# A transformer step on one core: more jobs in flight in attention, another SiLU, fillers and small vector work moved, three expert loads together

## The chip, the cores and the metric

The kernel runs on one core of one Trainium2 chip. The core has TensorE (PE), VectorE (DVE), ScalarE (ACT), GpSimd (POOL) and SyncE (SP, which issues most DMAs), sixteen DMA engines, an on-chip memory with 128 partitions, and eight accumulator banks that TensorE writes. The metric is the device time of one launch in microseconds (us).

## What is computed

One layer of a hybrid decoder in float32, for a prompt of 512 tokens and 8 sequences of 4 new tokens (32 "sample" tokens; 544 in all), model width 1024. The parts that the change touches:

```python
mod = (c @ w_ada + b_ada)[:, None, :]
sh1, sc1, gt1, sh2, sc2, gt2 = jnp.split(mod, 6, axis=-1)
h = x * (1.0 + sc1) + sh1
(qkv_a, z_a, b_a, a_a, q_b, k_b, v_b, f_b, g_a, g_b) = _split_cols(h @ w_in, IN_SIZES)
out = xp[:, 0:n] * w[0]                      # _causal_conv, 4 taps, 1536 channels
for i in range(1, CONV_WIDTH):
    out = out + xp[:, i:i + n] * w[i]
return jax.nn.silu(out), xp[:, n:]
...
q_a = _l2norm(q_a.reshape(hs)) * GDN_HEAD_DIM ** -0.5
k_a = _l2norm(k_a.reshape(hs))
o_a, ssm_new = _gdn_chunked(q_a, k_a, v_a, beta, g, ssm0.astype(f32), chunk)
o_a = _rmsnorm(o_a, norm_g.astype(f32)) * jax.nn.silu(z_a.astype(f32).reshape(hs))
o_b = _fox_prompt(q_b, k_b, v_b, logf)       # softmax(q.k/sqrt(d) + F_t - F_s), causal, 8 heads
merged = jax.nn.sigmoid(g_a) * (o_a @ w_ba) + jax.nn.sigmoid(g_b) * (o_b @ w_bb)
x = _layernorm(DEEPNORM_ALPHA * x + gt1 * (merged @ w_out), ln1_g, ln1_b)
h2 = x * (1.0 + sc2) + sh2
ffn = _moe(h2, ...)                          # 64 experts, top 8 by groups, and a shared one
x = _layernorm(DEEPNORM_ALPHA * x + gt2 * ffn, ln2_g, ln2_b)
```

## The kernel before

The program is a sequence of stages (blocks); in each, every engine has a list of work of its own, and counters (semaphores) join them. An engine runs its list in order, so what stands first in a list holds what stands behind it.

- **FoX prompt (163.5 to 340 us).** 32 jobs (`JOBS`), one per query block t and head h. `scores(j)` writes a bank (two score banks, 0 and 1), VectorE adds the mask and takes the row maximum (L789, L790), ScalarE does the exponential (L812), TensorE transposes the result (L727), ScalarE copies that back, and TensorE multiplies by v. Scores run two jobs ahead (`scores(j + 2)`). Between them TensorE makes the projection for the convolution's channel blocks (`projection`, L615), one of 128 channels every four jobs. For block m, ScalarE copies the input halves (`conv_in`, L659 to L661), VectorE runs the taps in four parts during the next four jobs (`conv_part`, L680 to L686), ScalarE applies SiLU in the last of these (`conv_silu`, L663 to L667), TensorE transposes the rows at job 4m + 1 of two blocks later (`conv_rows`), and VectorE takes them (`take_rows`). These products go through three banks in turn (5, 6, 7). In iteration j, VectorE's list is: maximum of j, then a convolution part.
- **FoX sample (340 to 487.5).** Attention of the sample tokens over cached pages.
- **Norms (487.5 to 511.8).** VectorE squares and sums q and k of the convolution, ScalarE takes a root, VectorE scales; TensorE has a few small products and the transposes of the convolution's state.
- **GDN (511.8 to 868).** Four blocks t of 128 tokens. Each: four transposed operands (L1251, copied by L1421), decay rows, an inverse in six levels l (`NL`), and the state update. TensorE's waits are filled with 80 "later pieces" (`later_pieces`): halves over k of the products for the branch gates ga and gb (L1196, eight matmuls each), and rows for the second modulation. Each place in the list takes a fixed count of them: two before the state, one after the transposes, one per level and two at l = 4, and so on, 20 per block. Their weights come in twelve loads of 2 MB ("slabs", `load_later` and `send_later`) into two slots; ScalarE copies each result (`later_out`) and stores the gates in DRAM. GpSimd and VectorE also run the sample tokens' recurrence here, until about 700.
- **Gated norm (868 to 887.5).** VectorE normalises and gates, TensorE transposes (L1561). The weights of both branches, x and half of the out-projection weights are asked for at its start (L1575 to L1579).
- **Branches (887.5 to 958).** For 8 blocks m of 128 channels, TensorE makes branch product a and b (16 matmuls each, L429) into four pairs of banks, ScalarE applies the sigmoid to gates read back from DRAM (L1695; two buffers), VectorE multiplies (L1722 to L1724). Ahead of m = 2 stands `later_modulation` (L1705 to L1709 for prompt and sample, ten operations) and three small ones.
- **Out-projection, layernorm, routing, shared expert (958 to 1134).** VectorE adds biases to two pairs of gate rows (L2337) ahead of its first layernorm, whose first reading of the out-projection is L2341.
- **Experts (to 1720).** 64 experts by rank of load in groups ("units"), weights of 3 MB each in four slots (`load_by_rank`), gathered rows, `gate_up` (L1846) and `down_half` (L1854). SyncE asks for rank 0, waits for the lists and the first gather, and asks for ranks 1 and 2.

## Time and profile before

| | us |
|---|---|
| median of 3 runs | 1792.89 (1791.1 to 1795.9) |
| the profiled execution | 1793.59 |
| its span, first to last instruction | 1791.8 |
| TensorE busy | 1585.4 (88%) |
| VectorE busy | 655.8 (37%) |
| ScalarE busy | 331.0 (18%) |
| GpSimd busy | 311.4 (17%) |
| mean granted TensorE clock, share of 2.4 GHz | 0.937 |

The profile is one execution; its times are us from the first instruction. The table of stretches gives busy times, the clock and the DMA share per stage; the list of waits and a line's own rows say for what an engine stood idle; the timeline joins equal instructions in a row into one line with their count. The idle time before an instruction and what ended it stand in brackets. The granted clock has two levels here, 1.00 (2.4 GHz) and 0.50 (1.2 GHz); a number between is a mean.

### The profile page before, as it was taken

Reading aid. Unit: us, or ns where it says so; the run is one execution under the profiler, and the core shown is the slowest. Engines: PE = TensorE matmul, PEld = TensorE weight load, DVE = VectorE, ACT = ScalarE, POOL = GpSimd, SP = SyncE. Lnnn points to the kernel's source line nnn. Section 1 sums busy time; section 2 is a strip of 40 time slices with the busy share of each in tenths; the row PEclk is TensorE's granted clock in tenths of the full one; section 3 lists DMA queues with packets and bytes.
Section 4 is the critical chain, followed back from the end, with each engine's and each line's share of the span. In section 5 each row is a group of like instructions: output and inputs, shape, how many; then the busy total and the mean of one; then the engine's idle time right before and its main releaser. Section 6 shows DMA issues by size and latency. Waiting matters only on the chain. (4 is left out here: it accounts for less than half of the span.)

```text
span 1791.8 us, 20650 instructions
## 1 busy us (share of the span) xinstructions
PE 1585.4 (88%) x7886; PEld 908.6 (51%) x7886; DVE 655.8 (37%) x1245; ACT 331.0 (18%) x662; POOL 311.4 (17%) x328
## 2 busy tenths in 40 slices
PE   5998888999957989999687998889989999998966
PEld 2856665664446767778474543333433434343322
DVE  2001333343278393533453884341111111111128
ACT  1001233433222121212110130011111111111120
POOL 5000000000029992000000052111111111111000
PEclk8997899999978999999798998999999999999988
DMA  9213110112141223321654002999999999999856
GB/s 340 91 47 101 26 48 1 48 48 79 70 108 38 81 87 105 113 86 44 228 195 159 35 16 75 368 422 405 419 414 419 381 404 422 397 418 420 346 206 261
DMA packets 111678, 357.13 MB, mean 199 GB/s; under 512 B 36011, under 2 KB 36139, under 8 KB 85459
## 3 DMA queue, kind: packets, MB, share of 16 engines
q1 hardware_dynamic: 88582, 304.08, 44.1%
q0 software_dynamic: 14384, 35.89, 5.1%
q10 hardware_dynamic: 8614, 15.84, 2.5%
q8 instruction: 64, 1.05, 0.3%
q14 instruction: 34, 0.28, 0.0%
HBM read 330.70 MB, written 37.64 MB: 206 GB/s over the span
## 5 line engine op out<-in xcount | busy, mean ns | idle before, releaser
L1846 PE MATMUL bank<-arena 128*32 128x512 f32 (+2 forms) x1536 | 336.2, 616 | 27.9 <-DMA arena<-in_w_up 27.7
L1846 PEld LDWEIGHTS bank<-arena 128*32 128x32 f32 (+2 forms) x1536 | 121.2, 138 | 210.4 <-issue 210.4
L1854 PE MATMUL bank<-arena 128*32 128x512 f32 (+2 forms) x768 | 168.7, 598 | 0.7 <-DVE arena L2540 0.7
L1196 PE MATMUL bank<-arena 128*128 128x272 f32 x512 | 129.4, 403 | 20.2 <-PEq L1058 19.2
L2534 DVE TENSOR_TENSOR arena<-arena,bank 128x256 f32<-128x256 f32 x46 | 19.4, 421 | 331.2 <-ACT arena L2212 331.2
L437 PE MATMUL bank<-arena 128*128 128x512 f32 (+4 forms) x384 | 126.8, 490 | 9.8 <-DVE arena L2341 7.5
L429 PE MATMUL bank<-arena 128*128 128x272 f32 x512 | 124.1, 407 | 11.3 <-DVE arena L1723 5.4
L1833 POOL DMA_INDIRECT expert_rows<-arena x46 | 46.4, 1008 | 482.0 <-PE bank L1839 427.0
L429 PEld LDWEIGHTS bank<-arena 128*128 128x128 f32 x512 | 101.0, 198 | 33.7 <-issue 6.1
L1196 PEld LDWEIGHTS bank<-arena 128*128 128x128 f32 x512 | 95.4, 193 | 44.5 <-issue 21.8
L1854 PEld LDWEIGHTS bank<-arena 128*32 128x32 f32 (+2 forms) x768 | 54.9, 134 | 110.7 <-issue 109.8
L615 PE MATMUL bank<-arena 128*128 128x272 f32 x384 | 108.1, 430 | 0.0
L437 PEld LDWEIGHTS bank<-arena 128*128 128x128 f32 (+1 forms) x384 | 60.7, 192 | 74.0 <-issue 65.3
L615 PEld LDWEIGHTS bank<-arena 128*128 128x128 f32 x384 | 76.4, 209 | 18.5 <-issue 3.6
L2212 ACT ACTIVATE arena<-bank 128x256 f32<-128x256 f32 x46 | 17.7, 384 | 353.6 <-PE bank L1846 353.6
L1356 DVE TENSOR_TENSOR arena<-arena 128x512 f32<-128x512 f32 x48 | 78.2, 1630 | 1.6
L2546 DVE COPY arena<-bank 128x512 f32<-128x512 f32 x46 | 31.8, 691 | 128.0 <-PE bank L1854 128.0
L1490 POOL TENSOR_TENSOR arena<-arena 128x512 f32<-128x512 f32 x5 | 6.8, 1354 | 344.3 <-POOLq L1058 344.0
L2270 POOL DMA_INDIRECT expert_lists<-arena x34 | 35.5, 1045 | 159.2 <-DVE arena L2394 149.8
L1280 PE MATMUL bank<-arena 128*128 128x128 f32 x320 | 47.4, 308 | 11.9 <-DVE arena L1391 7.9
L1829 POOL DMA_INDIRECT arena<-h_rows,arena x46 | 46.5, 1012 | 55.7 <-PE bank L1970 30.3
L2218 ACT COPY arena<-bank 128x512 f32<-128x512 f32 x46 | 27.0, 587 | 148.9 <-PE bank L1854 148.9
(427 smaller groups left out, 2084.3 us busy)
## 6 DMA issues: line engine op xcount, KB each, us to landing
arena<-in_w_gate SPq DMA_DIRECT2D x64, 1024.0 KB, 13.4
arena<-in_w_up SPq DMA_DIRECT2D x64, 1024.0 KB, 17.7
arena<-in_w_down SPq DMA_DIRECT2D x64, 1024.0 KB, 15.4
arena<-in_w_ada SPq DMA_DIRECT2D x12, 2048.0 KB, 9.3
arena<-in_w_in SPq DMA_DIRECT2D x11, 2048.0 KB, 9.1
arena<-expert_rows SPq DMA_DIRECT2D x8, 2048.0 KB, 25.8
gate_logits<-arena ACTq DMA_DIRECT2D x16, 272.0 KB, 3.3
arena<-gate_logits SPq DMA_DIRECT2D x8, 544.0 KB, 5.7
```

Of the source, the lines that this page charges most:

```text
L429: mm = nc.tensor.matmul(pair[i][:, 0:HALF], w[:, k, m * P:(m + 1) * P], rhs[:, k, i * HALF:(i + 1) * HALF], start=k == 0, stop=k == kt - 1)
L437: mm = nc.tensor.matmul(out, lhs[:, k, t * P:t * P + n], w[:, k, cols], start=k == 0, stop=k == kt - 1)
L615: mm = nc.tensor.matmul(out[:, 0:HALF], w[:, k, (m % 4) * P:(m % 4 + 1) * P], hT[:, k, half * HALF:(half + 1) * HALF], start=k == 0, stop= ...
L1196: mm = nc.tensor.matmul(out[:, 0:HALF], w[:, k, m * P:(m + 1) * P], hT[:, k, half * HALF:(half + 1) * HALF], start=k == 0, stop=k == KD - 1)
L1280: mm = nc.tensor.matmul(bank[hb][:, col(h)], Lm[:, h, :], Tm[:, h, :], start=True, stop=True)
L1356: done(lm_done, nc.vector.tensor_tensor(Lm_of[l % 2][:, hs, :], LT[:, hs, :], lvl[:, l, :].unsqueeze(1).to_broadcast([P, 4, P]), ALU.mult))
L1829: return nc.gpsimd.indirect_dma_start(out=into, out_offset=None, in_=h2_d, in_offset=bass.IndirectOffsetOnAxis(ap=rows, axis=0), bounds_ch ...
L1833: return nc.gpsimd.indirect_dma_start(out=y_d, out_offset=bass.IndirectOffsetOnAxis(ap=rows, axis=0), in_=of, in_offset=None, bounds_check ...
L1846: mm = nc.tensor.matmul(out[rows].rearrange("p (a n) -> p a n", a=2), x[:, k, rows], gate_up_slot(n)[:, :, k, :], start=k == 0, stop=k == ...
L1854: mm = nc.tensor.matmul(out[rows, :], h[:, k, rows], down_slot(n)[:, k, 512 * half:512 * half + 512], start=k == 0, stop=k == 1)
L2270: scat.inc(nc.gpsimd.indirect_dma_start(out=list_rows, out_offset=bass.IndirectOffsetOnAxis(ap=adi[:, t, k:k + 1], axis=0), in_=tokval[:, ...
L2546: nc.vector.tensor_copy(Yb[u % RY][:, 512:D], bank[6][:, :]).then_inc(y_v.sem, 1)
```

## The change

1. FoX prompt: three score banks (0, 1, 7), scores three jobs ahead; the other products go through two banks. The SiLU of blocks 0 to 5 is made as (tanh(y) + 1) · y with y half the convolution: ScalarE halves the taps of these blocks once and runs a tanh, VectorE multiplies. Block 6 keeps SiLU, at the stage's end. `conv_rows` moves one job on.
2. Norms: this block now holds 12 of the 80 pieces, and SyncE sends slab 2 from there, behind a wait for slab 1's last piece. The GDN blocks lose three pieces each.
3. Branch b's weights are loaded during GDN, and its products m = 0 and 1 are made in the gated-norm stage.
4. `later_modulation` is split into six portions, one behind each of m = 1 to 6.
5. The second pair of gate biases is added behind the second layernorm.
6. The loads of ranks 1 and 2 follow rank 0's at once.

```diff
+    conv_e, conv_th = at(T2 + 6096, TOK), Tick(nc, "conv_tanh")
+    HALVED = len(JOBS) // 4 - 2
+    def conv_tanh(act, m):
+        act.wait_ge(conv_sum.sem, m + 1)
+        if m:
+            act.wait_ge(conv_act.sem, m)
+        ach.inc(nc.scalar.activation(conv_e[:, 0:SEQ], post[m % 2], ACT.Tanh))
+        conv_th.inc(nc.scalar.activation(conv_e[:, SEQ:TOK], post_s[:, m, :], ACT.Tanh))
+    def conv_gate(dve, m):
+        step = chained(dve, vch)
+        dve.wait_ge(conv_th.sem, m + 1)
+        step(nc.vector.scalar_tensor_tensor(post[m % 2], conv_e[:, 0:SEQ], 1.0, post[m % 2], ALU.add, ALU.mult))
+        done(conv_act, nc.vector.scalar_tensor_tensor(post_s[:, m, :], conv_e[:, SEQ:TOK], 1.0, post_s[:, m, :], ALU.add, ALU.mult))
...
-    RING = (5, 6, 7)
+    RING, SB = (5, 6), (bank[0], bank[1], bank[7])
...
             for j, (t, h) in enumerate(JOBS):
-                if j + 2 < len(JOBS):
-                    scores(j + 2)
+                if j + len(SB) < len(JOBS):
+                    scores(j + len(SB))
...
-                if j % 4 == 1 and m >= 2:
+                if j % 4 == 2 and m >= 2:
                     conv_rows(pe, m - 2, RING)
...
                 if m >= 1:
                     conv_part(dve, m - 1, j % 4)
+                if m >= 2 and j % 4 == 1:
+                    conv_gate(dve, m - 2)
                 if m >= 2 and j % 4 == 3:
                     take_rows(dve, m - 2)
...
+            taps = histT[:, 0:HALVED, NH:NH + CONV]
+            hist_half.inc(nc.scalar.mul(taps, taps, 0.5))
...
-                if j % 4 == 3 and m >= 1:
-                    conv_silu(act, m - 1)
+                if j % 4 == 0 and m >= 2:
+                    conv_tanh(act, m - 2)
                 if t and h == 4:
                     take_oT(t - 1)
             take_oT(PT - 1)
+            conv_silu(act, HALVED)
...
             cn_mm.inc(mm)
+            later_pieces(pe, "squares", 6)
+            later_pieces(pe, "norms", 6)
...
+            later_out(act, "squares")
             act.wait_ge(g_sb.sem, 1)
...
             sq_root.inc(nc.scalar.activation(ss, ss, ACT.Sqrt))
+            later_out(act, "norms")
...
             load_later(sp, 1)
+            sp.wait_ge(fill_mm.sem, slab_end[1])
+            load_later(sp, 2)
             sp.wait_ge(ab_done.sem, 1)
...
-                later_pieces(pe, (t, "state before"), 2)
+                later_pieces(pe, (t, "state before"), 1)
...
                 tr_mm.inc(mm)
-                later_pieces(pe, (t, "transposes"), 1)
                 pe.wait_ge(tr_sb.sem, t + 1)
...
-                    later_pieces(pe, (t, l), 2 if l == NL - 2 else 1)
+                    later_pieces(pe, (t, l), 1)
...
+            sp.wait_ge(stored.sem, stored.n)
+            branch_in[1].inc(sp.dma_start(wbb, A["w_branch_b"][0].rearrange("(k p) n -> p k n", p=P)), 16)
             for j in range(8, len(LATER)):
                 send_later(j)
...
                 n = TOKS[t]
+                if t == 0:
+                    pe.wait_ge(branch_in[1].sem, 16)
+                    yb_mm.inc(feature_major(wbb, 0, oTb, bank[4:6], CW))
+                    yb_mm.inc(feature_major(wbb, 1, oTb, bank[6:8], CW))
                 pe.wait_ge(on_done.sem, t + 1)
...
-            pe.wait_ge(branch_in.sem, 32)
+            pe.wait_ge(branch_in[0].sem, 16)
             for m in range(KD):
                 for w, tick, free, rhs, b0 in ((wba, ya_mm, ta_done, oTa, 0), (wbb, yb_mm, tb_done, oTb, 4)):
+                    if w is wbb and m < 2:
+                        continue
...
             for m in range(KD):
-                if m == 2:
-                    later_modulation()
...
                 step(nc.vector.tensor_tensor(mT[:, m, :], ta, tb, ALU.add))
+                if 1 <= m <= 6:
+                    later_modulation(m - 1)
+            sample_token_values()
...
             load_by_rank(sp, 0)
-            sp.wait_ge(lists_in.sem, 16)
-            sp.wait_ge(g_ld[0].sem, 16)
             load_by_rank(sp, 1)
             load_by_rank(sp, 2)
...
-                    for load, gate, bias in ((gtb_load, gtb, b_gt), (gt2_load, gt2b, b_gt2)):
-                        dve.wait_ge(load.sem, 48)
-                        for i, m in enumerate((P, NS_TOK)):
-                            done(gt_ready, TT(gate[0:m, i], gate[0:m, i], bias[0:m], ALU.add))
+                    add_gate_bias(gtb_load, gtb, b_gt)
...
             layernorm(1)
+            add_gate_bias(gt2_load, gt2b, b_gt2)
             choose(0)
```

A portion of `later_modulation` is two, two and one operations, first for the prompt rows and then for the sample rows.

## Rows read from the trace of the kernel before

**Rows 1.** Stages: length, busy time (instructions) of each engine, granted clock, DMA share, GB/s.
```profile
163.50:340.00 176.50, 156.32 (x676) 110.15 (x676) 59.39 (x148) 63.43 (x161) 3.79 (x12) 0.90 0.12 35
...
511.80:614.00 102.20, 87.97 (x584) 70.30 (x585) 69.62 (x57) 20.68 (x37) 84.94 (x51) 0.92 0.28 78
...
707.00:787.00 80.00, 77.58 (x577) 62.10 (x576) 33.83 (x56) 19.19 (x36) 0.00 (x0) 1.00 0.39 114
...
887.50:958.00 70.50, 63.02 (x256) 51.00 (x256) 32.66 (x53) 10.18 (x9) 2.76 (x16) 0.93 0.50 177
...
1134.00:1720.00 586.00, 553.32 (x2756) 228.49 (x2756) 114.65 (x287) 71.07 (x137) 89.47 (x89) 0.98 0.97 394
```

**Rows 2.** Page, section 5: line, operation, count, busy, mean ns, idle before.
```profile
L1846 PE MATMUL bank<-arena 128*32 128x512 f32 (+2 forms) x1536 | 336.2, 616 | 27.9 <-DMA arena<-in_w_up 27.7
```

**Rows 3.** Waits of TensorE from 163.5 to 340: total us, times, longest.
```profile
PE bank L727 <- ACT arena L812: 17.7, 7, 3.4
```

**Rows 4.** Timeline, FoX prompt stage: start us, us, engine, line, operation [idle before, releaser].
```profile
201.25 0.36 ACT L659 COPY arena<-bank 128x240 f32<-128x240 f32 x1 [4.13 <-PE bank L615]
...
203.81 0.42 DVE L790 TENSOR_REDUCE arena<-bank 128x1 f32<-128x256 f32 x1
...
204.16 1.28 ACT L812 ACT_TABLE_LOAD   x1
...
205.45 0.47 ACT L812 ACTIVATE arena<-bank,arena 128x256 f32<-128x256 f32 x1
...
206.07 0.69 PE L727 MATMUL bank<-arena 128*128 128x128 f32 x2 [3.44 <-ACT arena L812]
...
320.28 0.69 DVE L790 TENSOR_REDUCE arena<-bank 128x1 f32<-128x512 f32 x1
...
322.00 0.69 ACT L812 ACTIVATE arena<-bank,arena 128x512 f32<-128x512 f32 x1
```

**Rows 5.** Table by stretch again, behind the gap that ends at 206.07.
```profile
204.90:211.70 6.80, 5.63 (x16) 4.40 (x16) 1.89 (x5) 2.21 (x7) 0.00 (x0) 0.50 0.03 2
```

**Rows 6.** Timeline, end of the norms stage and start of the GDN stage.
```profile
504.91 6.26 DVE L1094 TENSOR_TENSOR arena<-arena 128x1024 f32<-128x1024 f32 x5
...
511.70 5.79 PE L1196 MATMUL bank<-arena 128*128 128x272 f32 x16 [19.22 <-PEq L1058]
```

**Rows 7.** Timeline, GDN: a later piece in block three, transposes of four.
```profile
755.79 3.83 PE L1196 MATMUL bank<-arena 128*128 128x272 f32 x16
...
792.73 2.05 PE L1256 MATMUL bank<-arena 8*128 8x128 f32 x16 [0.69 <-ACT arena L1421]
...
794.71 3.14 PE L1259 MATMUL bank<-arena 64*128 64x256 f32 x16
```

**Rows 8.** Timeline, branch stage (887.5 to 958).
```profile
887.47 0.88 SPq L1676 DMA_DIRECT2D arena<-gate_logits  x2
...
901.75 1.11 ACT L1695 ACTIVATE arena<-arena 128x1088 f32<-128x1088 f32 x1 [7.59 <-DMA arena<-gate_logits]
...
910.07 1.22 DVE L1705 TENSOR_TENSOR arena<-arena 128x1024 f32<-128x1024 f32 x1
...
924.16 31.74 PE L429 MATMUL bank<-arena 128*128 128x272 f32 x128 [5.36 <-DVE arena L1723]
```

**Rows 9.** Timeline, start of the out-projection stage.
```profile
970.53 2.47 DVE L2337 TENSOR_TENSOR arena<-arena 128x1024 f32<-128x1024 f32 x2 [12.84 <-DMA arena<-in_b_ada]
...
978.12 2.47 DVE L2337 TENSOR_TENSOR arena<-arena 128x1024 f32<-128x1024 f32 x2 [5.12 <-DMA arena<-in_b_ada]
...
981.37 16.56 PE L437 MATMUL bank<-arena 128*128 128x512 f32 x32 [7.50 <-DVE arena L2341]
...
998.04 0.69 DVE L2341 TENSOR_TENSOR arena<-bank,arena 128x512 f32<-128x512 f32 x1 [4.30 <-PE bank L437]
```

**Rows 10.** Before the experts: one stretch of the table, one row of SyncE's timeline.
```profile
1100.00:1120.00 20.00, 19.17 (x44) 6.87 (x42) 4.70 (x13) 1.31 (x4) 0.00 (x0) 0.93 0.00 1
...
1152.73 0.34 SPq L1762 DMA_DIRECT2D arena<-in_w_gate  x1
```

218 lines of the change are left out of this document (115 added, 103 removed).

## The prediction

> **What bounds the kernel now.** I read the table of stages first. In the FoX prompt stage (163.5 to 340) TensorE works 156.3 of 176.5 us at a mean clock of 0.90 [rows 1]: it sets the pace, so every gap in it is time, and so is its lower clock level. In the first GDN block (511.8 to 614) it works 88.0 of 102.2 us beside 69.6 us of VectorE and 84.9 us of GpSimd; in the third (707 to 787) it works 77.6 of 80.0 [rows 1]. So the first two blocks are set by chains between engines, and the last two by TensorE's own amount of work. The branch stage has 63.0 us of TensorE in 70.5 us. The experts stage moves data at a DMA share of 0.97, and TensorE waits there 27.7 us for weights [rows 1, 2]: transfers set it. Then I read the waits of TensorE, and a timeline around each.
>
> **FoX prompt stage.** TensorE waits seven times, 17.7 us, for an exponential [rows 3]. The timeline shows one. ScalarE copies the convolution's second input half at 201.25, VectorE starts that block's convolution from it (four operations) and only then takes the row maxima, whose end is 204.23. The exponential starts at 205.45, because the SiLU and two table loads stand before it; TensorE resumes at 206.07 after a gap of 3.44 us [rows 4]. The change takes the tables away: 205.45 − 204.23 less 0.04 of issue, 1.18 us here; in the last one 322.00 − 320.97 less 0.04, 0.99 [rows 4]. Over the six such places I get 5.85 us (0.47 to 1.26 each). The rest stays. Scores three jobs ahead do not shorten it, since the maxima still stand behind the convolution's first part in VectorE's own order, and this waits for ScalarE's copy. So gaps of 0.7 to 2.3 us remain.
>
> The gaps also cost clock. In 204.9 to 211.7, behind this one, the granted clock was 0.50, the 1.2 GHz level [rows 5]; six such stretches (3.4 us each but this) add to about 24 us, 12 us lost. The last gap of this kind, the shortest, was followed by none. I expect three of the six to remain, a gain of 6 to 8: 7 us. Against it: a row copy of 0.69 us and its wait now share an interval with a softmax maximum, 1 us; and the seventh block's SiLU stands alone at the end, 1.28 + 0.63 + 0.21, 2.1 us. The new VectorE work (0.74 + 0.25 per block) lies in intervals of some 5 us in which VectorE was a third busy [rows 1]. Halving the taps is one small ScalarE operation before any use. Sum: 5.9 + 7 − 1 − 2.1 = 10 us gain. Bounds: 4, if all clock stretches remain, and 14, if none does.
> The Trainium skill, "ScalarE: Activation LUTs", What ACT_TABLE_LOAD costs, puts each switch at 1283 ns plus a drain, together about 2.66 us; by it six places would give up to 8 us more, and the stage 18. The trace does not agree: the load of 204.16 takes 1.28 us and the exponential starts 0.01 us behind it [rows 4].
>
> **Norms and GDN.** TensorE stood idle for 19.22 us until 511.70, while VectorE went through the norms until 511.17, and the first two pieces then took 5.79 us at the low level, where 16 of them take 3.83 warm [rows 6, 7]. Twelve pieces now go in front: ten gate halves of eight matmuls at 1.83 (the 3.83 for 16, less the last one's drain), and a modulation product of eight with its single-matmul row piece, taken as 2.8 together; 21.1 us, plus 1.7 for a cold start, from 492.5. That ends at 515.3, 3.6 us after 511.7. ScalarE's root is 1 us later behind piece copies, so VectorE ends at 512.2, still first. The slab asked for at 487.5 lands after 11.6 us, in time for the fifth piece. SyncE now waits there for a slab's end before it sends its small stores; they land under these same pieces.
> What comes out of the GDN blocks is worth less than its length. The piece behind the transposes was wholly hidden: TensorE ended it and still waited 0.69 us for ScalarE's four copies [rows 7]. A piece alone lasts 2.0 with its drain, so without it the wait is 2.7 us, four times, at no time of its own. The second piece at the fifth level gives 1.83 in the last two blocks (TensorE-bound), nothing in the first two. One "state before" piece gives 1.0 in each of the last two, 2.3 in the first (5.79 becomes about 2.9 and the scaled rows are ready at 3.3), 0 in the second: 8.0 us. Idle of 2.7 us can drop the clock: for two or three of the four stretches, 1.7 us each, as in the last block, where L1259 took 3.14 us for 16 matmuls behind even the 0.69 us gap [rows 7], 4.1 in all. Net 3.9, so both stages together 3.9 − 3.6, about 0. Bounds −5 (clock drops at every shorter filler) and +5 (none).
> In SyncE's queue the branch-b weights (2 MB, landing in 9 us like the slabs there) now stand before slab 8. That slab then lands about 8 us before its first piece needs it: 0.
>
> **Gated norm.** TensorE has 14 us of idle there, up to 879.1. Two branch-b products take 2 × 16 × 0.23 = 7.4 us, up to 10.7 cold, from 868: they end beside the first transpose. I take 0.3 lost, bounds 0 and 1.
>
> **Branch stage.** Eight products run from the stage's start at 887.5, then TensorE waits 5.36 us until 924.16 for VectorE, which went through ten modulation operations of 1.2 us from 910.07; the other eight take 31.74 us, 1.7 of it for a cold start, so a product warm is 3.7 [rows 8]. The cause ahead of that is a DMA backlog: the first gates, asked for at 887.47, let ScalarE go on at 901.75 [rows 8], 14.3 us later, behind four loads of 2 MB. Now: two branch-a products, 7.4 us; 2 MB less are queued, 5 us, so the gates land 9 us into the stage; sigmoid and two products 2.0, so TensorE resumes at 11.1. Then twelve products of 3.7, 44.4; clock 1.7; end 2.1: 59.3 instead of 70.5, 11 us gained. Modulation portions (two operations, 2.5 us) beside a 2.6 us turn of VectorE fit into 7.4 us per channel group. If their inputs land late (VectorE would wait for them in its second turn), there are some 8 us before TensorE notices. Bounds: 9 (gates at their old delay of 14) and 15.5 (gates at once, warm).
>
> **Out-projection.** VectorE had the first gate bias pair done at 973.0, waited 5.12 us for the second load until 978.12 and added it until 980.6; only then it read the out-projection's banks, and TensorE resumed after a gap of 7.50 us, with 32 matmuls in 16.56 us, cold, where 13.7 is the warm time (32 at some 0.43). VectorE waited for them at 998.04 [rows 9]. With the second pair moved behind, the layernorm starts 7.6 us earlier, TensorE goes on without a gap and warm, and the bank that VectorE read at 998.04 is ready by 987.5: 10.2 us earlier. The pair itself costs 2.47 later, in a chain of VectorE that has no gaps from there: 7.7 us gained. Bounds 5 and 9.
>
> **Experts.** DMA rests from 1100 to 1120 [rows 10], when two experts more could be loading. But expert 4's load waits for a free slot until 1152.73 [rows 10], and the transfers in flight then had only 4.6 us to go. Anything earlier than that makes the DMA idle before 1152.7 instead: 4 us gained, bounds 2 and 5. The loads might delay small gathers of the routing; at 15 us of transfer in a 20 us hole they end first.
>
> **Sum.** 10 + 0 − 0.3 + 11 + 7.7 + 4 = 32.4 us. The profiled execution has a span of 1791.8 and took 1793.59; the median of the runs is 1792.9, 0.7 lower. 1793.6 − 32.4 = 1761.2.
>
> **Rivals.**
> (a) The moved pieces were the cover in GDN: TensorE gains nothing in the last two blocks and each of the four transposes and several levels drop the clock, and the FoX stage keeps all its stretches: 5 + 6 less, 1772. For it: 16.56 against 13.7 [rows 9] shows how dear a cold start is. Chance 0.13.
> (b) The pieces count fully: all twelve, 21 us out and 3.6 in, 17 gained: 1744. Against it: the 0.69 us of waiting behind the hidden piece. Chance 0.10.
> (c) The third score bank removes the whole wait in the FoX stage: 17.7 of gaps and 12 of clock, less 3: 27, 17 more than forecast, 1744. Against it: VectorE's order. Chance 0.08.
> (d) Tanh needs a table of its own, so that the loads stay: the stage loses 3 instead of gaining 10: 1774. No row shows a tanh. Chance 0.03. The Trainium skill, same page, Table sets, lists tanh in the exponential's set; no trace so far shows it.
> (e) Slower: with fillers gone from GDN, TensorE falls to the low level behind the transposes and does not come up again between the many short waits of the levels. At that level work takes twice as long (3.4 us of one stretch lose 1.7), so the sum is eaten up from 65 us spent there more than before; with a third of the four blocks (119 us) it costs 59: 1821. For it: the clock of the first block is already 0.92 [rows 1]. Against it: the third block ran at 1.00 with only one piece per level. Chance 0.04. The Trainium skill, "TensorE: Matmul & The Clock Gate", What's actually happening, says that the low level is the default and activity releases it, which speaks for such a fall; rows 5 agree, in 3 to 7 us pieces.
> (f) The gates or the modulation inputs come late, branch stage gains only 5: 1767. Chance 0.05.
>
> **How the numbers follow.** The forecast has the rest, 0.57, and its own range from the bounds is 1751 to 1772. With (a), (d), (f) above and (b), (c) below, 8 in 10 lie in 1743 to 1775. A measurement of this kernel tells from no change what is beyond 0.3%, 5.4 us. Faster by more: 0.95, within: 0.02, slower: 0.03.
>
> **What would show it.** FoX stage: no table loads but at its end, waits of TensorE for exponentials near 12 us in all, clock near 0.94. Norms stage some 27.9 us long. In GDN, waits of 2.7 us behind the transposes, and the first block no shorter than 98. Branch stage 57 to 60, one wait of TensorE near its start. Out-projection stage shorter by 7 to 8, no cold run of 32 matmuls. Load 4 issued with the DMA nearly idle. The prediction is wrong if GDN falls in clock, if VectorE's order does not hold the maxima, or if the gates land as late as before.

## The result and the profile after

The changed kernel takes 1784.95 us (1780.21 to 1785.43), the kernel before 1794.3 in the same set: a ratio of 0.9939, 95% interval 0.9922 to 0.9956. In two later sets with the same pair it was 0.9918 (0.9889 to 0.9947) and 0.9919 (0.9892 to 0.9945). So the change gains 0.6 to 0.8%, 9 to 13 us by the medians. I had forecast 1761.2, in a range of 1743 to 1775: the sign holds, the size is 0.3 to 0.4 of the 32.4 us forecast, and the time lies outside the range.

The profiled execution of the changed kernel (span 1783.4, 8.4 less than before) by stages. Columns as in rows 1; the stages are in order FoX prompt, FoX sample, norms, GDN, gated norm, branches, out-projection and routing, experts, end:

```profile
162.85:342.69 179.84, 162.96 (x676) 114.47 (x677) 64.72 (x160) 48.16 (x150) 3.78 (x12) 0.86 0.13 41
342.69:489.99 147.30, 146.32 (x652) 75.99 (x652) 46.65 (x123) 44.91 (x80) 0.00 (x0) 0.98 0.16 54
489.99:517.26 27.27, 26.43 (x130) 18.93 (x130) 20.67 (x22) 8.26 (x17) 0.00 (x1) 0.94 0.54 184
517.26:875.64 358.38, 312.19 (x2190) 249.17 (x2190) 186.44 (x217) 75.58 (x138) 150.72 (x89) 0.92 0.25 80
875.64:893.93 18.29, 13.19 (x52) 9.76 (x52) 14.45 (x22) 4.13 (x7) 0.00 (x1) 0.78 0.97 346
893.93:954.16 60.23, 55.15 (x225) 44.38 (x225) 32.67 (x53) 10.18 (x9) 2.76 (x16) 0.95 0.52 176
954.16:1125.23 171.07, 153.29 (x508) 70.53 (x509) 110.20 (x273) 26.48 (x44) 38.09 (x39) 0.94 0.33 121
1125.23:1707.51 582.28, 553.30 (x2750) 227.41 (x2748) 112.43 (x283) 69.83 (x136) 88.26 (x88) 0.98 0.95 389
1707.51:1783.40 75.89, 47.60 (x105) 19.40 (x104) 46.57 (x59) 12.54 (x39) 0.97 (x1) 0.83 0.67 270
```

Here and in the table below a stage runs from its first computing instruction to that of the next. In the same measure the kernel before has 177.2, 146.8, 24.2, 357.6, 18.1, 70.7, 178.0, 581.7 and 73.9. The differences are +2.6, +0.5, +3.0, +0.8, +0.2, −10.5, −6.9, +0.6 and +2.0; with 0.7 ahead of the first stage they make the 8.4. Two stages, branches and out-projection, gave nearly what was forecast (−11 and −7.7). The FoX prompt stage was to give 10 and cost 2.6; norms and GDN cost 3.8 where 0.3 was to be gained; the experts were to give 4 and gave nothing. These are differences of two profiles; the table of all runs below shows how far a stage moves with its code unchanged.

### The profile page after: what moved, and what is told of

It reads as the page before. It is cut to its first block and busy times, and to the rows that moved or that the text cites. A ratio compares the mean times of both kernels' runs of the same rounds, so it can differ in the third digit from the quotient of the medians.

```text
span 1783.4 us, 20662 instructions
## 1 busy us (share of the span) xinstructions
PE 1604.6 (90%) x7886; PEld 922.7 (52%) x7886; DVE 656.0 (37%) x1257; ACT 315.6 (18%) x651; POOL 310.3 (17%) x328
## 5 line engine op out<-in xcount | busy, mean ns | idle before, releaser
L429 PE MATMUL bank<-arena 128*128 128x272 f32 x512 | 125.5, 409 | 12.8 <-PEq L1272 4.3
L1130 PE MATMUL bank<-arena 128*128 128x272 f32 x512 | 128.5, 400 | 0.6 <-ACT arena L1166 0.6
L618 PE MATMUL bank<-arena 128*128 128x272 f32 x384 | 111.4, 440 | 0.0
L1390 DVE TENSOR_TENSOR arena<-arena 128x512 f32<-128x512 f32 x48 | 69.1, 1439 | 1.6
L1314 PE MATMUL bank<-arena 128*128 128x128 f32 x320 | 44.6, 295 | 10.6 <-DVE arena L1425 6.6
## 6 DMA issues: line engine op xcount, KB each, us to landing
arena<-in_w_up SPq DMA_DIRECT2D x64, 1024.0 KB, 17.7
```

What stands on the lines that cost most here:

```text
L429: mm = nc.tensor.matmul(pair[i][:, 0:HALF], w[:, k, m * P:(m + 1) * P], rhs[:, k, i * HALF:(i + 1) * HALF], start=k == 0, stop=k == kt - 1)
L618: mm = nc.tensor.matmul(out[:, 0:HALF], w[:, k, (m % 4) * P:(m % 4 + 1) * P], hT[:, k, half * HALF:(half + 1) * HALF], start=k == 0, stop= ...
L1130: mm = nc.tensor.matmul(out[:, 0:HALF], w[:, k, m * P:(m + 1) * P], hT[:, k, half * HALF:(half + 1) * HALF], start=k == 0, stop=k == KD - 1)
L1314: mm = nc.tensor.matmul(bank[hb][:, col(h)], Lm[:, h, :], Tm[:, h, :], start=True, stop=True)
L1390: done(lm_done, nc.vector.tensor_tensor(Lm_of[l % 2][:, hs, :], LT[:, hs, :], lvl[:, l, :].unsqueeze(1).to_broadcast([P, 4, P]), ALU.mult))
```

## Where the FoX prompt stage's gain went

The list of TensorE's waits in that stage of the changed kernel has, as the answer to rows 3:

```profile
PE bank L746 <- ACT arena L833: 11.6, 11, 2.3
...
PE bank L738 <- ACT arena L664: 1.2, 3, 0.6
```

17.7 us have become 12.8: at the six places 7.6 us of waiting went away, and seven new waits of 0.2 to 0.6 us brought 2.7 back. The 5.9 us forecast for the tables came in as 4.9. The timeline at the place of rows 4 shows how:

```profile
203.53 0.43 DVE L809 TENSOR_REDUCE arena<-bank 128x1 f32<-128x256 f32 x1
...
203.99 0.47 ACT L833 ACTIVATE arena<-bank,arena 128x256 f32<-128x256 f32 x1 [2.19 <-DVE arena L809]
...
204.61 0.69 PE L746 MATMUL bank<-arena 128*128 128x128 f32 x2 [2.25 <-ACT arena L833]
...
204.71 0.64 ACT L677 ACTIVATE arena<-arena 128x512 f32<-128x512 f32 x1
205.09 3.83 PE L618 MATMUL bank<-arena 128*128 128x272 f32 x8
```

The exponential now starts 0.03 us behind the maximum (203.96) and ScalarE is idle before it; the gap is 2.25 instead of 3.44, to 0.01 the 2.26 worked out. Between this exponential and the tanh at 204.71 there is no table load. The Trainium skill, "ScalarE: Activation LUTs", Table sets, has the exponential and tanh in one set; the trace agrees, with no load in the 0.72 us between the two starts.

But the projection's eight matmuls at 205.09 still take 3.83 us. The table of stretches for the granted clock:

```profile
203.80:217.50 13.70, 12.89 (x34) 9.38 (x34) 5.22 (x13) 3.41 (x12) 0.00 (x0) 0.50 0.03 2
...
289.10:292.60 3.50, 3.50 (x11) 2.55 (x9) 0.00 (x0) 0.00 (x0) 0.00 (x0) 0.51 0.00 0
296.00:302.80 6.80, 5.54 (x18) 4.61 (x18) 5.46 (x12) 3.15 (x8) 0.00 (x0) 0.50 0.01 2
```

The stretch at 1.2 GHz behind the gap at 206 was 6.8 us long before [rows 5]; behind the shorter gap it is 13.7 us in this profile. That length isn't a property of the change: the same code has it in two profiles (changed and yg_undo, described below), and in the five others the stretch is 3.5 us or less, as in control2, the changed kernel unedited in another set:

```profile
206.50:210.00 3.50, 3.12 (x8) 2.51 (x9) 2.69 (x7) 1.65 (x7) 0.00 (x0) 0.51 0.04 2
```

What six of the seven share is elsewhere. The low stretches near 250 and 300 last some 7 us where before they lasted 3 to 3.5, and three stand where before had none: near 290, near 323, and some 2 us at the stage's end. Of the six that I wanted to get rid of, one, near 273, is gone. At 289.1 the level fell while TensorE was busy: its last wait had ended 16 us earlier. The stage's mean clock is 0.86 against 0.90 [rows 1]. For the same 676 matmuls TensorE is busy for 163.0 us against 156.3 (160.1 to 162.8 in the six other profiles), and it stands idle for 16.9 us against 20.9. So the idle time shrank by 4.0 us, and the busy time grew by 4 to 7.

## The experiments

Each kernel is the changed kernel with one edit, unless it says otherwise. Stage lengths are of its profile, in us; "low" is 2 × (1 − mean clock) × length of the FoX prompt stage, the time at 1.2 GHz that its mean clock stands for (this counts also the stage's start, low for its first 10 to 11 us, in control and best2 for 17). Each stage length is of one profile: a difference of 3 us in the FoX prompt stage is within what the same code shows.

| kernel | FoX prompt (low) | norms + GDN | branches | out-proj., routing | experts | ratio to before (95%) |
|---|---|---|---|---|---|---|
| before | 177.2 (35) | 381.8 | 70.7 | 178.0 | 581.7 | 1 |
| changed | 179.8 (50) | 385.6 | 60.2 | 171.1 | 582.3 | 0.9939 (0.9922, 0.9956) |
| control | 179.7 (50) | 385.6 | 59.8 | 177.8* | 582.0 | 0.9918 (0.9889, 0.9947) |
| control2 | 177.3 (43) | 385.7 | 59.4 | 171.1 | 582.1 | 0.9919 (0.9892, 0.9945) |
| silu3 | 187.2 (56) | 383.1 | 59.8 | 179.8* | 586.1 | 0.9911 (0.9883, 0.9940) |
| tanh2 | 179.8 (47) | 383.8 | 59.9 | 179.5* | 585.3 | 0.9919 (0.9891, 0.9946) |
| a_undo | 186.0 (52) | 382.8 | 59.6 | 179.7* | 582.7 | 0.9949 (0.9929, 0.9969) |
| a_undo2 | 176.9 (35) | 384.0 | 59.3 | 170.3 | 585.1 | 0.9904 (0.9874, 0.9934) |
| silu3_rb | 178.2 (43) | 383.1 | 59.5 | 170.0 | 585.1 | 0.9895 (0.9852, 0.9939) |
| d_undo | 176.9 (42) | 379.2 | 59.9 | 180.4* | 582.3 | 0.9882 (0.9852, 0.9911) |
| d_keep | 177.0 (42) | 379.0 | 60.2 | 180.4* | 582.0 | 0.9892 (0.9866, 0.9917) |
| hf_undo | 177.2 (43) | 385.6 | 69.2 | 178.1* | 582.4 | 0.9943 (0.9922, 0.9964) |
| yg_undo | 178.3 (43) | 382.7 | 64.0 | 176.3 | 585.0 | 0.9996 (0.9980, 1.0012) |
| projfirst | 162.0 (19) | 384.2 | 59.5 | 180.0* | 583.3 | 0.9867 (0.9824, 0.9909) |
| before_pf | 157.8 (19) | 378.9 | 71.8 | 178.4 | 582.1 | 0.9878 (0.9841, 0.9914) |
| best | 161.7 (19) | 363.9 | 59.7 | 170.5 | 582.5 | 0.9755 (0.9723, 0.9786) |
| best2 | 167.4 (30) | 365.1 | 60.0 | 170.1 | 582.0 | 0.9760 (0.9727, 0.9793) |
| pf_silu | 161.6 (26) | 376.5 | 62.1 | 170.3 | 583.3 | 0.9762 (0.9735, 0.9789) |

The star marks profiles with a stall of 6.3 us of TensorE at one place of the routing, told of at the end. The runs were made in five sets, each with the kernel before in it, the last four on four different chips. The stall came in all eight kernels of the second and third set and in none of the other profiles, and the kernel before took 1805.1 and 1803.9 us there, 1794.3 to 1796.4 in the other sets. So kernels are compared by total only within a set or by their ratio, and by this stage only with or without the stall.

**control.** The changed kernel, unedited.

> The changed kernel once more, unedited, on the chip of the three that follow, to know which of its stages hold still. The first profile had 179.8 us in the FoX prompt stage and 171.1 in the out-projection and routing stage; four edited kernels whose edits lie elsewhere had 177.0 to 187.2 and 179.5 to 180.4 there. Theory A (these stages differ by where thin stretches and instruction supply fall, not by the edits): one of the two moves here by 3 us or more. Theory B (the edits moved them): both repeat within 1 us.

FoX prompt repeated (179.7), the routing stage was 6.7 us longer, by the stall. So theory A, for one of the two stages. That FoX prompt came out equal is luck: here the start was low for 17 us instead of 10, and the stretch behind the gap at 206 lasted 3.5 instead of 13.7.

**control2.** The same in the last set.

> The changed kernel once more beside these: FoX prompt stage 177.0-179.8, out-projection and routing 171 or 178, ratio to before 0.989-0.996.

All three expectations held. FoX prompt 177.3: the same code of this stage has 176.9 to 179.8 in seven profiles (changed, the two controls, d_undo, d_keep, hf_undo, yg_undo).

**silu3** and **tanh2**, the two sides of the stage's change:

```diff
-                if m >= 2 and j % 4 == 1:
-                    conv_gate(dve, m - 2)
...
-                if j % 4 == 0 and m >= 2:
-                    conv_tanh(act, m - 2)
+                if j % 4 == 3 and m >= 1:
+                    conv_silu(act, m - 1)
```
```diff
-    RING, SB = (5, 6), (bank[0], bank[1], bank[7])
+    RING, SB = (5, 6, 7), (bank[0], bank[1])
```

> The changed kernel with the SiLU of the kernel before (on ScalarE, with its two table loads per block) and whole taps, but three score banks and scores three jobs ahead. The FoX prompt stage took 177.2 us before and 179.8 in the changed kernel, although TensorE waited 5.3 us less. Theory A (the tanh shortens the waits, something else costs clock): waits of TensorE for exponentials go back from 11.6 to 16-18 us, and the low clock (24 us before, 40 in the changed kernel) stays near 40 if the third score bank and the pair of banks for the rest cause it: stage 183-187. Theory B (the tanh with VectorE's extra work is what costs clock): low clock back to some 24 us, stage 176-178.

> The changed kernel with two score banks, scores two jobs ahead, and three banks in turn for the rest, as before; the tanh stays. Theory A (third score bank costs the clock): waits for exponentials near 12 us, low clock at or under 24 us, stage 168-173 us. Theory B (the tanh costs it): low clock near 40 us, stage 178-181. Theory C (the clock falls by where a thin stretch of TensorE's work happens to lie, no part of the change owns it): somewhere between, 172-178, and silu3 between as well.

With SiLU the stage is 187.2, low 56, and the waits for exponentials are 17.5 us: theory A's numbers, so the tanh isn't what costs clock. (This profile is the longest of silu3's four executions, 1799.5 us, where the others took 1785.3 to 1791.1; so 187.2 may be high.) Yet without the third bank (tanh2) it is 179.8 with 47: not its theory A, 168 to 173, but theory B's number, 178 to 181, by which the tanh costs the clock. The two answers contradict each other as long as tanh and bank are the only suspects. What the two kernels have in common is `conv_rows` one job later.

**a_undo** undoes both at once but leaves `conv_rows` in its new place; **a_undo2** moves this back as well; **silu3_rb** moves it back with three score banks:

```diff
-                if j % 4 == 2 and m >= 2:
+                if j % 4 == 1 and m >= 2:
                     conv_rows(pe, m - 2, RING)
```

> The changed kernel with the FoX prompt stage of before: two score banks, three banks in turn, SiLU; all else changed. Theory A (the stage's changes gave nothing, the clock took it back): stage 176-178, total within 3 us of the control. Theory B (the stage as changed is worth 3-7 us and the first profile was unlucky): total 3-7 us above the control. The banks for scores, changed alone with SiLU, gave 187.2; with both undone the stage must be back at some 177.

> The changed kernel with the FoX prompt stage wholly as before: SiLU, two score banks and also conv_rows one job earlier, which the run a_undo had left in its new place. That one took 186.0 us, with 52 us of low clock, where before has 177.2 with 35, with the same seven waits. Theory A (the place of the row transposes decides how much low clock this stage has with SiLU): 177 us and 35 again. Theory B (the clock falls by the stage's start in time, whatever the order): 182 or more, or a number between.

> The changed kernel with SiLU and conv_rows in its old place, but with three score banks and two banks in turn for the rest. With SiLU and two score banks the stage has 176.9 us (35 us of low clock) with conv_rows in its old place and 186.0 (52) with it one job later; with three score banks and conv_rows later 187.2 (56). Theory A (the place of the row transposes costs it, the third bank nothing): 176-179 us, low 33-40. Theory B (two banks in turn instead of three also cost): 182-188.

a_undo missed its text: the stage should have been back at 177 and took 186.0. By the total it is theory B, 5.1 us above the control. a_undo2 is theory A, 176.9 and 35. silu3_rb is theory A by its length, 178.2, with 43 of low clock, above the 33 to 40 expected. The two FoX prompt stages, first a_undo, then a_undo2 (the stretches), then the waits for exponentials of both:

```profile
162.80:348.80 186.00, 163.57 (x676) 115.21 (x677) 59.40 (x148) 63.80 (x161) 3.78 (x12) 0.86 0.12 35
```
```profile
162.79:339.64 176.85, 155.63 (x676) 109.79 (x677) 59.39 (x148) 63.81 (x161) 3.79 (x12) 0.90 0.12 37
```
```profile
PE bank L745 <- ACT arena L830: 19.2, 11, 3.4
```
```profile
PE bank L745 <- ACT arena L830: 17.7, 7, 3.4
```

One line moved costs 9.1 us: 7.9 are TensorE's busy time at the lower clock, 1.5 are four new waits of 0.2 to 0.6 us. The seven waits that both have agree to 0.01 us, and both stages start at 162.8 (theory B, the stage's start in time, is out). silu3 against silu3_rb is the same edit with three score banks, and shows 9.0. The totals say so less sharply: 0.9949 against 0.9904 for the first pair, 0.9911 against 0.9895, within their intervals, for the second.

Where the clock goes can be seen in a_undo:

```profile
299.20:316.40 17.20, 17.20 (x55) 11.55 (x55) 2.80 (x6) 2.79 (x7) 0.00 (x0) 0.70 0.00 1
```

TensorE is busy all of this time, and yet the level is low in three parts of it, until 302.8, from 306.3 to 309.5 and from 312.9 to 316.3. In a_undo2 the same work, with four transposes of `conv_rows` in it, runs at the full clock from 299.3 on.

So in the order in which it can be built the stage's change splits into the third bank, +1.3 (not told from noise), the row transposes later, +9.0, and the tanh, −7.3 to −10.2 (silu3 to the changed kernel's 179.8 to 176.9; −6.2 from a_undo to tanh2). The tanh needs the later place, because its rows are finished one job later, on VectorE. So the price of the place is measured with SiLU; that it is the same with the tanh isn't shown. Nor is it settled why the level falls again and stays low longer with the row transposes there.

**projfirst.** What the wait needs is other work:

```diff
+                m = j // 4
+                if j % 4 == 0:
+                    projection(pe, m, 0, 0, RING)
                 if j + 1 < len(JOBS):
                     prob_transposes(j + 1)
-                m = j // 4
-                projection(pe, m, j % 4 // 2, j % 2, RING)
+                if j % 4:
+                    projection(pe, m, j % 4 // 2, j % 2, RING)
```

> The changed kernel with one order changed: in every fourth job of the FoX prompt stage TensorE makes the projection's eight matmuls (2 us) ahead of the transposes of the next job, in the place where it waits for the exponential behind VectorE's first convolution part. Theory A (VectorE's order holds the maximum, and the wait only needs other work): the waits of 2.3, 2.3, 2.1 and 1.9 us there vanish, low clock falls from 42-50 us to 15-25, stage 164-170 us. Rival (the low clock comes from thin work such as transposes and 64-column matmuls, not from the waits): the waits vanish and the low clock stays above 35 us, stage 172-175.

162.0 us, low 19: theory A, 2 us below its range. Its timeline at the place shown above, and its waits:

```profile
201.36 2.10 PE L618 MATMUL bank<-arena 128*128 128x272 f32 x8
...
202.61 0.42 DVE L812 TENSOR_REDUCE arena<-bank 128x1 f32<-128x256 f32 x1
...
203.06 0.47 ACT L836 ACTIVATE arena<-bank,arena 128x256 f32<-128x256 f32 x1 [2.19 <-DVE arena L812]
...
203.68 0.44 PE L746 MATMUL bank<-arena 128*128 128x128 f32 x2 [0.22 <-ACT arena L836]
```
```profile
PE bank L746 <- ACT arena L836: 5.3, 10, 1.2
```

The same eight matmuls stand in the gap, at the full clock (2.10 us instead of 3.83), and 0.22 us of it are left. The rival, by which the low clock comes from thin work and not from the waits, wanted 172 to 175 us with more than 35 us low, and is out as the main cause; that the level also falls without a wait is the row of a_undo above.

**before_pf** is the kernel *before* with this edit alone.

> The kernel before with one edit: the projection's eight matmuls ahead of the transposes in every fourth job. Nothing of the change is in it. Theory A (the wait had to be filled, not shortened): FoX prompt stage 161-163 us (177.2 before), other stages as before (GDN 354-360, branches 70-71, out-projection 177-180), ratio to before 0.990-0.993. Rival (part of the 15 us came from tanh or from the third bank): stage 165-170.

```profile
161.26:319.10 157.84, 150.60 (x676) 104.62 (x676) 59.40 (x148) 63.74 (x161) 3.78 (x12) 0.94 0.14 42
```

157.8 us and a ratio of 0.9878, both below theory A's ranges: one reordered call in the kernel before does more than the whole change (0.9919 in the same set; before_pf's four executions took 1771.2 to 1778.2 us, control2's five 1781.3 to 1784.3). With the wait filled, tanh, third bank and the moved rows together are worth nothing: 161.7 and 162.0 with all three (best, projfirst), 157.8 and 161.6 with the stage's code as before (before_pf and, below, pf_silu). Those two have the same code there, so 4 us apart is noise. best2, with the tanh and without the third bank, has 167.4.

**d_undo** and **d_keep**, the later pieces:

```diff
-            later_pieces(pe, "norms", 6)
+            later_pieces(pe, "norms", 2)
...
                 tr_mm.inc(mm)
+                later_pieces(pe, (t, "transposes"), 1)
```

(this is d_keep; ScalarE's `later_out` for the piece comes back with it, and d_undo has all 80 pieces in GDN.)

> The changed kernel with the later pieces as before: none in the norms stage, 20 per GDN block. Norms 27.3 now, GDN 358.4 now; before 24.2 and 357.6. Theory A (pieces moved out of GDN bought nothing there because the clock fell behind the uncovered transposes): norms 24.2, GDN 356-359, in all 3-5 us less than the changed kernel, and low-clock stretches behind the transposes of blocks 2 and 3 gone (17 us at 617-634 and 7 us at 719-726 now). Rival (the clock moves by chance with the start of each stage): GDN anywhere from 353 to 364, with low stretches of 10 us or more in block 2 or 3 too.

> The changed kernel with 8 instead of 12 pieces in the norms stage, and one piece again behind each of the four transposes of GDN (state-before 1, fifth level 1, as in the changed kernel). Theory A (the cover behind the transposes holds the clock): norms 24-25 us, GDN 349-354, in all 8 us or more less than the changed kernel's 385.7. Rival (pieces count by their length wherever they stand): GDN 365, norms 24-25, in all 4 us more.

Both stages together: 379.2, 379.0, and 385.6 for the change. d_undo is theory A, and better than its ranges (GDN 354.6, 6.4 us less in all): the 17 us stretch in block 2 is 7 us long, and the one in block 3 is gone. Over all runs the two stages with the changed pieces have 382.7 to 385.7 us (eleven profiles), with the pieces as before 378.9 to 381.8 (before, before_pf, d_undo). d_keep's total of 6.6 us less misses the 8 of its theory A; its rival had 4 more. The third block's transposes in the changed kernel, then in d_keep:

```profile
714.48 1.94 PE L1286 MATMUL bank<-arena 128*128 128x128 f32 x16 [0.75 <-DVE arena L1443]
716.45 2.44 ACT L1455 COPY arena<-bank 128x512 f32<-128x512 f32 x4 [2.30 <-PE bank L1286]
718.94 3.55 PE L1290 MATMUL bank<-arena 8*128 8x128 f32 x16 [2.52 <-ACT arena L1455]
722.42 3.77 PE L1293 MATMUL bank<-arena 64*128 64x256 f32 x16
```
```profile
713.25 2.00 PE L1130 MATMUL bank<-arena 128*128 128x272 f32 x8
713.45 2.44 ACT L1456 COPY arena<-bank 128x512 f32<-128x512 f32 x4 [2.24 <-PE bank L1286]
715.94 2.05 PE L1291 MATMUL bank<-arena 8*128 8x128 f32 x16 [0.69 <-ACT arena L1456]
717.92 2.00 PE L1294 MATMUL bank<-arena 64*128 64x256 f32 x16
```

The wait of 2.5 us is there as forecast (2.7), and behind it the next 32 matmuls take 7.3 us instead of 4.1: 3.2 for one uncovered place. The third and the fourth block, first of the control, then of d_keep:

```profile
714.00:793.20 79.20, 74.63 (x540) 60.20 (x540) 33.10 (x54) 18.30 (x34) 0.00 (x0) 0.96 0.20 67
793.20:875.20 82.00, 73.73 (x540) 58.28 (x540) 29.63 (x49) 18.40 (x35) 0.00 (x0) 0.92 0.12 43
```
```profile
711.50:787.50 76.00, 73.28 (x548) 59.23 (x548) 33.10 (x54) 18.30 (x34) 0.00 (x0) 1.00 0.32 116
787.50:866.40 78.90, 72.50 (x548) 57.29 (x548) 29.64 (x49) 18.69 (x35) 0.00 (x0) 0.96 0.13 45
```

3.2 and 3.1 us less with eight matmuls *more* in each: theory A for GDN (352.5, within its range). The 5.9 us that GDN gains from changed to d_keep are these two blocks; the first two together have 197.1 in the control and 197.6 in d_keep. The norms stage was off: 26.5, not 24 to 25. VectorE ended at 511.78 there and the next stage began at 513.9, because SyncE waits for the slab's last piece before it sends the small stores for which the stage's end waits. I had named that queue and put it at nothing; with twelve pieces it is covered by their own length. In best, below, the stores go first, and the stage is 25.1.

**hf_undo** puts the ten modulation operations back in one block and the two waits back ahead of expert ranks 1 and 2.

> The changed kernel with two parts undone in stages far apart, each read by its own stage: the ten modulation operations stand again in one block ahead of the third channel group of the branch stage (60.2 us in the changed kernel), and expert ranks 1 and 2 are again asked for only after the lists and the first gather. Branch stage: if VectorE's block was worth what I put it at, 5.4 us or more, it is 65-67; if the earlier gates and weights did the whole, 60-62. Experts (582.3 and 582.0 to 582.3 in kernels on the same chip as it): theory A (expert 4's load, held by its slot, sets the pace, so the early loads bought nothing) within 1 us of the control; theory B (they bought the 4 us forecast) 585-587.

```profile
925.83 24.36 PE L429 MATMUL bank<-arena 128*128 128x272 f32 x92 [8.33 <-DVE arena L1770]
```

The branch stage is 69.2, above both expectations: the block costs 9.4 us against the control, not 5.4. With the gates earlier TensorE runs into it sooner and waits 8.33 instead of 5.36 [rows 8]. Experts: the two kernels have

```profile
1131.09:1713.04 581.95, 553.16 (x2750) 227.62 (x2748) 112.44 (x283) 69.82 (x136) 88.31 (x88) 0.98 0.96 389
```
```profile
1138.86:1721.26 582.40, 551.33 (x2750) 226.91 (x2748) 112.47 (x283) 69.82 (x136) 88.30 (x88) 0.98 0.97 395
```

(control, then hf_undo): 0.4 us apart. Theory A. Over all runs this stage has 581.7 to 582.4 us with the loads as before (before, before_pf, hf_undo) and 582.0 to 586.1 with the early loads (fifteen profiles): never less. The loads were early in the changed kernel, and then the transfers rested:

```profile
1133.00:1143.00 10.00, 9.07 (x45) 3.48 (x43) 1.54 (x3) 0.97 (x2) 0.00 (x0) 1.00 0.32 108
```
```profile
1143.48 0.34 SPq L1808 DMA_DIRECT2D arena<-in_w_gate  x1
```

Expert 4's load is issued 16.5 us after the first expert's matmul in before, control and hf_undo alike, and 18.3 after it in the changed kernel's first profile. In the code this load waits for the unit that last used its slot, however early the data came.

**yg_undo** puts branch b's first two products back into the branch stage and the second gate bias back ahead of the first layernorm.

> The changed kernel with two parts undone, each read by its own stage: branch b's first two products stand again in the branch stage (their weights still come early), and the second pair of gate biases again ahead of the first layernorm. Branch stage 59.8 in the control: the two products cost 7.4 us of TensorE, but this fills the wait for the gates; theory A (the gates hold the start) 59.8 plus 3-5; rival (all of the 7.4 shows) 67. Out-projection and routing stage 171 to 180 in six runs with the change: by its beginning alone (the wait of 7.5 us and the cold 16.6 us) undone it is 7 us longer up to the second layernorm, which is what I read.

```profile
955.02 13.97 PE L437 MATMUL bank<-arena 128*128 128x512 f32 x32 [2.70 <-PEq L1673]
978.19 7.32 PE L437 MATMUL bank<-arena 128*128 128x512 f32 x13 [9.20 <-DVE arena L2382]
```

Branch stage 64.0, 3.8 to 4.6 more than in the three profiles of the changed kernel: theory A. The gap in the out-projection is back, 9.2 us long, and the stage 5.2 to 6.3 us longer than in the seven profiles with the change and without the stall; I had expected 7. By its total (0.9996) nothing is left of the gain: these two parts are worth as much as the whole change.

**best** joins projfirst and d_keep, and sends the small stores ahead of SyncE's wait:

```diff
-            sp.wait_ge(fill_mm.sem, slab_end[1])
-            load_later(sp, 2)
             sp.wait_ge(ab_done.sem, 1)
...
             stored.inc(sp.dma_start(A["conv_sample"][0].rearrange("b i c -> (b i) c"), cnew_rows[n:n + NH, :]), 16)
+            sp.wait_ge(fill_mm.sem, slab_end[1])
+            load_later(sp, 2)
             sp.wait_ge(stored.sem, stored.n)
```

> The changed kernel with three edits together: the projection ahead of the transposes in every fourth job (FoX prompt stage 162.0 us alone, 177 to 180 without), one piece again behind the four transposes of GDN and 8 instead of 12 in the norms stage (379.0 us for both stages, 385.6 without), and SyncE sends the small stores of the norms stage ahead of its wait for the slab (in the run with 8 pieces the next stage began 2 us after VectorE's last operation). Theory A (each holds in its own stage): FoX 162, norms 24.5-25, GDN 352-353, ratio to the kernel before 0.977-0.981. Rival (moving stages against each other moves the clock, so that gains do not add): one of the three is 4 us or more worse than alone.

> The kernel called best with two score banks and three banks in turn for the rest. Theory A (the third score bank is worth nothing): FoX prompt stage 161-163 us and a ratio within 0.5% of best's 0.9755. Rival (it lets the scores pass a wait): stage 165 or more.

> The kernel called best with the whole FoX prompt stage as before the change (SiLU, two score banks, conv_rows one job earlier), but with the projection ahead of the transposes. It prices what tanh and the third bank are worth once the wait has other work in it. By the rows of before the wait was 3.4, 2.8, 2.9, 2.2, 2.4, 1.7 us; 2.0 us of matmuls in front leave 1.4, 0.8, 0.9, 0.2, 0.4, 0. Theory A (tables still cost what is left): stage 165-170. Rival (the tanh and the bank are worth nothing once the wait is filled): 161-164.

best takes 1749.93 us (1745.87 to 1755.24) beside 1795.85 for before: 0.9755 (0.9723 to 0.9786), below the 0.977 to 0.981 of its theory A. It beats both kernels. FoX prompt 161.7 and norms 25.1 are as expected; GDN is 338.9 where 352 to 353 was expected, 13.4 us less than in pf_silu (352.2), which has the same GDN code:

```profile
163.94:325.68 161.74, 151.10 (x676) 105.20 (x676) 64.72 (x160) 48.23 (x150) 3.78 (x12) 0.94 0.14 45
473.76:498.85 25.09, 19.92 (x105) 14.47 (x105) 20.67 (x22) 6.91 (x14) 0.00 (x0) 0.93 0.55 186
498.85:837.70 338.85, 305.02 (x2216) 243.58 (x2216) 182.23 (x217) 76.69 (x141) 148.89 (x89) 0.96 0.28 86
```

The 13 us lie in the first two blocks, where VectorE and GpSimd work at once: they take 185.5 us in best and 198.9 in pf_silu; the last two take 153.3 in both. d_keep, with the same GDN code, is like pf_silu (352.5), best2 like best (340.5). So no edit in GDN made it. The profile of best is its shortest execution and that of pf_silu its longest (1759.8 us, the others 1753.0), and by their medians the two are 3 us apart. best2's FoX prompt stage took 167.4, the number of its rival; some 3 us of its distance to best are a start low for 17 us, which the unedited control has too, and whether the third bank is worth the rest beside the tanh stays open. By its total, 0.9760, best2 isn't told apart from best. pf_silu gave 161.6: the rival's number, tanh and bank together are worth nothing in a filled wait.

## Why the prediction was wrong, point by point

Against the forecast the profile is 24.0 us short (8.4 instead of 32.4). The FoX prompt stage makes 12.6 of it, the experts 4.6, norms and GDN 3.8, the branches and the out-projection 1.3, and the rest, 1.7, lies almost all in stages that were not to change.

- **Tables out of the wait (5.9).** Right in size: 17.7 became 12.8, and the gap at the place shown 2.25, as worked out. That VectorE's order holds the rest was right as well.
- **Clock of the FoX stage (+7).** The step that failed. I took the low stretches as consequences of the gaps, one each, and struck out three of six. The gaps did become shorter, and the low time grew from 35 us to 42 to 50 (seven profiles): one of the six stretches went, two doubled, three came where no stretch had been. For the same matmuls TensorE was busy 4 to 7 us longer where 7 less was forecast. a_undo against a_undo2 shows 9.1 us for a line that changes hardly any wait. Even the bound "4, if all clock stretches remain" was too high: by its own terms, 5.9 − 1 − 2.1, it is 2.8, and it did not allow for more low time, so it should have lain below nothing. 10 forecast, −2.6 measured in this profile, −2.5 in the control and −1.0 to +0.3 in the five others of the same code. The reason why the level falls there stays open.
- **conv_rows one job later (1 us).** The second half of the same mistake: I priced what VectorE has to do for it and not where TensorE's matmuls come to stand. With SiLU it costs 9.0 us.
- **SiLU alone at the end (2.1 us).** Right: the wait at the stage's end grew from 1.1 to 3.0 us.
- **Norms (+3.6).** +3.0: right.
- **GDN (−3.9).** +0.8 against the profile of before; d_undo and before_pf, with all pieces in GDN, have 354.6, so up to +3.8. That the piece behind the transposes was hidden, and that the wait without it is 2.7 us, was right. I had put the clock at 1.7 us for two or three places; a place costs 3.2, since the low stretch behind it is some 7 us long and not 3.4 (in the last two blocks; the first two show no gain in d_keep). Rival (a) named this mechanism and the FoX stage's too, at 1772; the experts' term and the row transposes, which it did not have, make most of the rest. And "at no time of its own" was the wrong reading of hidden work: with it the clock stayed up, as d_keep shows.
- **Gated norm (+0.3).** +0.2: right.
- **Branches (−11).** −10.5, and TensorE resumed 10.9 us into the stage (904.82), 11.1 forecast; but it had no idle there, as its 32 matmuls took 10.6 us cold, and the later wait of 2.10 us, at 921.86, for the third gates, was not in my sum. The sum came out right by luck, with its parts mis-sized: the block of modulation was worth 9.4 and the early products 3.8 to 4.6. Together this is more than 10.5; that each hides part of the other is my reading, as no run undoes both.
- **Out-projection (−7.7).** −6.9; by yg_undo 5.2 to 6.3 of it are the moved bias. The term has a slip: TensorE's end at 997.93 against 987.5 is 10.4 us and not 10.2, which makes 8.0.
- **Experts (−4).** +0.6. This term failed by its mechanism too. I took a DMA share of 0.97 for the bound and let a lead of 4.6 us of transfers reach the end. The loads are a closed ring of slots: each waits for a unit of TensorE four loads earlier, so after an early start the transfers rest until a slot is free. The condition stood in my own text ("expert 4's load waits for a free slot").
- **Rival (e), slower by a fall of the clock in GDN**, did not come: the low level took up 57 us there against 36, not 119 more.

## What to carry to other kernels

Fill a wait of TensorE with work that is ready before shortening what it waits for: one call moved ahead of the transposes gave 15 to 19 us where tanh, a third bank and new VectorE work, together, gave none. Before a part of TensorE's list is moved, even by one place and with hardly any wait changed, build that move alone: here one line cost 9 us. Work that is "hidden" behind another engine's copies may be what holds TensorE's clock; before moving it, price the next matmuls at half speed, and let the bounds go below zero. And before one profile's stage is explained, profile the same kernel again: the most striking stretch of this one, 13.7 us, was 3.5 in the next. A queue at a share of 0.97 is not the bound if each of its loads waits for a slot that another engine frees.

## What the runs showed of the hardware

**The clock level follows more than gaps.** Two FoX prompt stages with the same seven gaps, one with four small ones of 0.2 to 0.6 us besides, differ by 17 us of low level (52 and 35) when four transposes per block stand one job later. In a_undo the level fell at 306.3 and at 312.9, with no wait of TensorE between 298.5 and 326.

**A stall of TensorE that no kernel owns.** 64 very short matmuls of the routing (L1993) took 1.12 us in one profile of the changed kernel and 7.46 in the control, the same kernel in another set; the control's timeline:

```profile
1057.55 0.30 PE L1993 MATMUL bank<-arena 128*32 128x64 f32 x3 [0.49 <-issue]
1058.97 0.32 PE L1993 MATMUL bank<-arena 128*32 128x64 f32 x4 [1.11 <-issue]
```

It waited for nothing that the profile shows, three or four matmuls at a time. All eight kernels of the second and third set had it (7.4 to 7.6 us), the other ten profiles 1.1. The kernel before was not profiled in those sets; its total was 7 to 11 us longer there. That it is the supply of instructions is my reading; no run varied it.

**VectorE's operations last longer beside GpSimd's, and by how they meet.** The same 48 operations of VectorE (128 x 512, GDN) in before, best and d_keep:

```profile
L1356 DVE TENSOR_TENSOR arena<-arena 128x512 f32<-128x512 f32 x48 | 78.2, 1630 | 1.6
```
```profile
L1394 DVE TENSOR_TENSOR arena<-arena 128x512 f32<-128x512 f32 x48 | 62.5, 1302 | 1.6
```
```profile
L1391 DVE TENSOR_TENSOR arena<-arena 128x512 f32<-128x512 f32 x48 | 78.1, 1627 | 1.6
```

One takes 0.69 us in the median and up to 4.1 beside GpSimd's work. The Trainium skill, "SBUF — State Buffer", SBUF: two separate sides, says that the two engines share a pair of ports as an exclusive lock held for a whole instruction (VectorE for an operation with two inputs in this memory, as here); the durations agree, as GpSimd's operations of 128 x 2048 there take 3.6 to 5.8 us. The first two GDN blocks take 184 to 199 us with the same code in best2, best, d_keep and pf_silu, and these operations 63.4, 62.5, 78.1 and 69.3 us in the same order: so they can be part of the difference and not the whole of it, as the longest blocks don't go with the longest operations.
